# Two-layer decoder step on one core: the second root of four norm pairs moves from the tokens to the finished tiles of the projection that follows

## The reference, cut to what matters

```python
def rmsnorm(x, g):
    return x * lax.rsqrt(jnp.mean(x * x, -1, keepdims=True) + EPS) * g
# layer l
x = x + rmsnorm(m, norm_mix_post[l])            # m: what the mixer gave
h = rmsnorm(x, norm_x_pre[l])
x = x + rmsnorm(cross_attend(h, mem_k, mem_v, wq, wo), norm_x_post[l])   # q = h @ wq
h = rmsnorm(x, norm_ffn_pre[l])
f = swiglu(h, wg, wu, wd)                       # (silu(h @ wg) * (h @ wu)) @ wd, layer 0
x = x + rmsnorm(f, norm_ffn_post[l])
h = rmsnorm(x, norm_mix_pre[l + 1])
# mixer of layer 1
q, f, i, g = split(h @ w_in, 4)
fg = lb + (1 - lb) * sigmoid(f);  qh = silu(q);  kh = 1 - fg;  lf = log(fg)
bc = cumsum(lf);  q_in = qh * exp(bc);  k_in = kh * exp(-bc)   # in chunks of 64 tokens
```

## Time and profile before

| | |
|---|---|
| median of three runs | 2251.37 us |
| profiled execution, device time | 2249.11 us |
| span of its trace, first to last instruction | 2246.8 us |
| mean granted clock of TensorE | 0.922 of full speed |
| TensorE busy | 2047.6 us |
| VectorE busy | 1494.1 us |
| ScalarE busy | 1218.5 us |
| GpSimd busy | 132.8 us |

### The profile page before, as it was taken

One profiled execution on the slowest core, in us unless ns is written; L12 is line 12 of the kernel. 1 busy time (PEld: TensorE's weight loads), 2 busy tenths in 40 slices (PEclk: granted clock), 3 DMA queues, 4 the chain that ended last, 5 costly groups with the idle time before them and its releaser, 6 DMA issues.

```text
span 2246.8 us, 29766 instructions
## 1 busy us (share of the span) xinstructions
PE 2047.6 (91%) x10660; PEld 1667.6 (74%) x10660; DVE 1494.1 (66%) x2113; ACT 1218.5 (54%) x1620; POOL 132.8 (6%) x160
## 2 busy tenths in 40 slices
PE   7999998888899978797987899999999999999993
PEld 6774647757799878746656688888888888888882
DVE  2413734562655354475544799999999999999994
ACT  3321213433444435313323788888878788887883
POOL 2000300000000000041000000000000000000001
PEclk9999997888899988768877899999999999999996
DMA  6324665364455473244542999999999999999991
GB/s 155 117 95 157 216 199 197 114 206 149 132 176 172 141 267 127 85 131 174 187 164 72 384 379 375 373 374 381 373 380 366 382 370 388 368 385 370 382 370 68
DMA packets 234941, 556.03 MB, mean 247 GB/s; under 512 B 10534, under 2 KB 13826, under 8 KB 234854
## 3 DMA queue, kind: packets, MB, share of 16 engines
q1 hardware_dynamic: 213422, 474.87, 59.2%
q0 software_dynamic: 21440, 80.07, 10.5%
HBM read 525.38 MB, written 29.62 MB: 247 GB/s over the span
## 4 chain that ended last, share of the span: by engine, by line
PE 78%; DVE 11%; DMA 5%; ACT 3%; issue 2%; POOL 1%; DVEq 0%; ACTq 0%; POOLq 0%
PE banks L1320 9%; PE banks L1322 9%; PE banks L1321 9%; PE banks L793 6%; PE banks L794 5%; PE banks L795 5%; PE banks L763 5%; PE banks L823 5%; PE banks L1313 5%; PE banks L1311 5%; PE banks L1312 5%; PE banks L844 2%; DVE arena L1978 1%; DVE weight_parts L1703 1%; PE banks L1330 1%
## 5 line engine op out<-in xcount | busy, mean ns | idle before, releaser
L2270 DVE TENSOR_TENSOR weight_parts<-arena,weight_parts 128x1024 fp32r<-128x1024 f32 x672 | 799.9, 1222 | 64.3 <-ACT weight_parts L1653 32.7
L1653 ACT ACTIVATE weight_parts<-arena 128x1024 fp32r<-128x1024 f32 x672 | 700.9, 1061 | 141.3 <-PE banks L1322 90.5
L1320 PE MATMUL banks<-weight_parts,token_parts 128*128 128x512 f32 x896 | 356.2, 398 | 6.3 <-DVE weight_parts L2270 6.3
L1322 PE MATMUL banks<-weight_parts,token_parts 128*128 128x512 f32 x896 | 350.1, 391 | 0.0
L1321 PE MATMUL banks<-weight_parts,token_parts 128*128 128x512 f32 x896 | 349.7, 390 | 0.0
L793 PE MATMUL banks<-token_parts,weight_parts 128*128 128x264 f32 x992 | 295.2, 298 | 48.9 <-DVE token_parts L1737 16.7
L1703 DVE TENSOR_TENSOR weight_parts<-arena,weight_parts 128x1024 fp32r<-128x1024 f32 (+1 forms) x158 | 186.2, 1195 | 193.2 <-ACT weight_parts L1357 177.1
L1357 ACT ACTIVATE weight_parts<-arena 128x1024 fp32r<-128x1024 f32 (+1 forms) x158 | 162.8, 1037 | 275.9 <-PE banks L795 195.0
L794 PE MATMUL banks<-token_parts,weight_parts 128*128 128x264 f32 x992 | 292.6, 295 | 0.0
L795 PE MATMUL banks<-token_parts,weight_parts 128*128 128x264 f32 x992 | 291.9, 294 | 0.0
L793 PEld LDWEIGHTS banks<-token_parts,weight_parts 128*128 128x128 f32 x992 | 198.2, 200 | 52.8 <-DVE weight_parts L1703 29.0
(11 more groups left out here) (441 smaller groups left out, 2443.8 us busy)
## 6 DMA issues: line engine op xcount, KB each, us to landing
arena<-in_moe_w_gate SPq DMA_DIRECT2D x112, 1024.0 KB, 7.6
arena<-in_moe_w_up SPq DMA_DIRECT2D x112, 1024.0 KB, 8.0
arena<-in_moe_w_down SPq DMA_DIRECT2D x112, 1024.0 KB, 7.4
arena<-in_ev_w_in SPq DMA_DIRECT2D x18, 1024.0 KB, 5.0
arena<-in_cache_mem_k POOLq DMA_DIRECT2D x16, 1024.0 KB, 6.0
arena<-in_cache_mem_v POOLq DMA_DIRECT2D x16, 1024.0 KB, 5.4
arena<-in_od_w_in SPq DMA_DIRECT2D x16, 1024.0 KB, 5.9
arena<-in_ffn_w_gate SPq DMA_DIRECT2D x10, 1024.0 KB, 5.1
```

What stands on the lines that cost most here:

```text
L1320: mm(out, xh, hi[:, cols], start=(c == 0), stop=False)
L1322: last = mm(out, xl, hi[:, cols], start=False, stop=(c == DC - 1))
L1653: f(wr_[:, q % QRING, 0, :], quarter(q), ACT.Copy).then_inc(S("hi_made"), 1)
L2270: TT(wr_[:, q % QRING, 1, :], quarter(q), wr_[:, q % QRING, 0, :].bitcast(F32), ALU.subtract) \
```

## The change

At the four pairs the second root is no longer multiplied into the tokens. The parts of the tokens are made from X times gain, without the root, as soon as X is updated: ScalarE makes the high part beside the square of the chunk, and VectorE the low part with one operation, X times gain less the high part. The projection multiplies these, and since the root is one number per token, it multiplies the finished tile instead: VectorE now empties the tiles of `q`, `gate`, `up`, `f`, `q`, `i` and `g` with a multiplication by the root (`times_rs`). Where an activation follows, ScalarE applies it to the emptied tile (`activate`). In the feed-forward the root belongs in two places, ahead of SiLU and on the product, so VectorE multiplies a gate tile by it once more after SiLU. The sums of squares of the second norm stand inside the projection: two chunks after the first quarter of its first column block, two after the second quarter, four ahead of the last quarter.

```diff
-            plan(f"q{l}", 8), plan(f"qs{l}", 2), ...
+            plan(f"q{l}", 8, "v"), plan(f"qs{l}", 2), ...
-                plan("f", 8), plan("q", 8), plan("i", 8), plan("g", 8)
+                plan("f", 8, "v"), plan("q", 8, "v"), plan("i", 8, "v"), plan("g", 8, "v")
@@ TensorE
-            def project_split(name, cols, hi_x, lo_x, ready=None, chunks=DC):
+            def project_split(name, cols, hi_x, lo_x, ready=None, chunks=DC, sums=None):
...
+                        if sums is not None and c0 == 0 and k0 == 6:
+                            square_sum(sums, 4), square_sum(sums, 5), square_sum(sums, 6), square_sum(sums, 7)
                         pe.wait_ge(lo_made, q + 1)
...
+                        if sums is not None and c0 == 0 and k0 < 4:
+                            square_sum(sums, k0), square_sum(sums, k0 + 1)
...
-                square_sums(k_pre)
-                project_split(f"q{l}", D, token_hi, token_lo, parts_of(f"q{l}"))
+                project_split(f"q{l}", D, token_hi, token_lo, parts_of(f"q{l}"), sums=k_pre)
...
@@ ScalarE
+            def activate(x, fn, name, c):
+                act.wait_ge(empty["v"], emptied(n_of(name, c))[1])
+                f(x, x, fn).then_inc(S("activated"), 1)
...
             def squares_of_x(k):
                 for c in range(DC):
                     act.wait_ge(S("x_updated"), DC * posts.index(k - 1) + c + 1)
+                    if k in SPLIT_NORMS:
+                        f(x_hi[:, c, :], XT[:, c, :], ACT.Copy, scale=gain(kind, layer, c)).then_inc(S("x_hi_made"), 1)
                     f(MT[:, c, :], XT[:, c, :], ACT.Square).then_inc(S("squares_ready"), 1)
...
             def attention(l, k_post, k_pre):
+                first_hi(f"q{l}")
                 root(k_post)
                 squares_of_x(k_pre)
-                first_hi(f"q{l}")
+                hi_ahead(n_of(f"q{l}", 0), 2)
                 root(k_pre)
-                input_hi(k_pre)
-                for c in range(DC):
-                    b = tile(n_of(f"q{l}", c))
-                    f(QT[:, c, :], b[:, 0:T], ACT.Copy, scale=(D // XH) ** -0.5).then_inc(empty["a"], 1)
+                hi_ahead(n_of(f"q{l}", 7))
...
+            for c in range(DC):
+                hi_ahead(n_of("f", c))
+                activate(Fg[:, c, :], ACT.Sigmoid, "f", c)
             act.wait_ge(S("fg_ready"), 1)
             f(Fg, Fg, ACT.Ln).then_inc(S("logf_ready"), 1)
-            for c in range(DC):
-                b = tile(n_of("i", c))
-                f(I[:, c, :], b[:, 0:T], ACT.Copy).then_inc(empty["a"], 1)
+            hi_ahead(n_of("f", 7), 4)
             act.wait_ge(S("bc_ready"), 1)
...
+            for c in range(DC):
+                hi_ahead(n_of("q", c))
+                activate(Q[:, c, :], ACT.Silu, "q", c)
...
@@ VectorE
                 link(v.reciprocal(rs, rs))
+                if k in SPLIT_NORMS:
+                    return
...
+                        if c >= 3 and k + 1 in SPLIT_NORMS:
+                            dve.wait_ge(S("x_hi_made"), PARTS[SPLIT_NORMS[k + 1]] + c - 2)
+                            STT(out=x_lo[:, c - 3, :], in0=XT[:, c - 3, :], scalar=gain(next_kind, next_layer, c - 3),
+                                in1=x_hi[:, c - 3, :].bitcast(F32), op0=ALU.mult, op1=ALU.subtract).then_inc(S("x_lo_made"), 1)
+            def times_rs(name, c, out):
+                b = tile(n_of(name, c))
+                return TT(out, b[:, 0:T], rs, ALU.mult)
...
+                first_lo(f"q{l}")
                 finish_norm(k_post)
-                first_lo(f"q{l}")
+                lo_through(f"q{l}", 0)
                 finish_norm(k_pre)
-                lo_through(f"q{l}", 7)
+                for c in range(DC):
+                    b = tile(n_of(f"q{l}", c))
+                    STT(out=QT[:, c, :], in0=b[:, 0:T], scalar=(D // XH) ** -0.5, in1=rs, op0=ALU.mult, op1=ALU.mult) \
+                        .then_inc(empty["v"], 1)
...
+            for i, n in enumerate(FGROUPS):
+                for j in range(n):
+                    times_rs(f"gate{i}", j, gtmp[j]).then_inc(empty["v"], 1)
+                for j in range(n):
+                    lo_through(f"gate{i}", 3 if n == 4 else 1, 2)
+                    dve.wait_ge(S("activated"), 4 * i + j + 1)
+                    TT(gtmp[j], gtmp[j], rs, ALU.mult).then_inc(S("dve_step"), 1)
...
+            for c in range(DC):
+                times_rs("f", c, Fg[:, c, :]).then_inc(empty["v"], 1)
+            dve.wait_ge(S("activated"), FC + DC)
...
+            for c in range(DC):
+                times_rs("q", c, Q[:, c, :]).then_inc(empty["v"], 1)
+            lo_through("q", 7, 4)
             dve.wait_ge(S("e_ready"), 1)
...
```

More of the change, by code:

```diff
@@ L455, in program @@
         posts = [n for n, (_, _, pre) in enumerate(NORMS) if not pre]
-        PRES = [n for n, (_, _, pre) in enumerate(NORMS) if pre]
+        NORMED = [n for n, (_, _, pre) in enumerate(NORMS) if pre and n not in SPLIT_NORMS]
         block = ctx.enter_context(nc.Block())
@@ L837, in transposes, with square_sum @@
                 last.then_inc(tile_done, 1)
+            def square_sum(k, c):
+                pe.wait_ge(S("squares_ready"), DC * k + c + 1)
+                sq = MT if NORMS[k][2] else HT
+                last = mm(ps[:, 4, 0:T], ones, sq[:, c, :], start=(c == 0), stop=(c == DC - 1))
+                if c == DC - 1:
+                    last.then_inc(S("square_sums_done"), 1)
             def square_sums(k):
                 for c in range(DC):
-                    pe.wait_ge(S("squares_ready"), DC * k + c + 1)
-                    sq = MT if NORMS[k][2] else HT
-                    last = mm(ps[:, 4, 0:T], ones, sq[:, c, :], start=(c == 0), stop=(c == DC - 1))
-                last.then_inc(S("square_sums_done"), 1)
+                    square_sum(k, c)
             def wait_norm(k, chunks=DC):
-                pe.wait_ge(S("normed"), DC * PRES.index(k) + chunks)
+                pe.wait_ge(S("normed"), DC * NORMED.index(k) + chunks)
             pe.wait_ge(S("consts_ready"), 1)
@@ L1135, in attention @@
                 square_sums(k_pre + 1)
-                square_sums(k_pre + 2)
+                if l == 1:
+                    square_sums(k_pre + 2)
             attention(0, 1, 2)
             for i, n in enumerate(FGROUPS):
-                project_split(f"gate{i}", n * P, token_hi, token_lo, parts_of("gate0") if i == 0 else None)
+                project_split(f"gate{i}", n * P, token_hi, token_lo, parts_of("gate0") if i == 0 else None, sums=4 if i == 0 else None)
                 project_split(f"up{i}", n * P, token_hi, token_lo)
@@ L1144, in _ @@
             square_sums(5)
[L1145 to L1147 removed]
+            project_split("f", D, token_hi, token_lo, parts_of("f"), sums=6)
             project_split("q", D, token_hi, token_lo)
@@ L1544, in attention @@
                 block_out(f"xo{l}")
-                root(k_pre + 1)
                 if l == 0:
                     first_hi("gate0")
+                root(k_pre + 1)
                 squares_of_x(k_pre + 2)
+                if l == 0:
+                    hi_ahead(n_of("gate0", 0), 2)
                 root(k_pre + 2)
-                if l == 0:
-                    input_hi(k_pre + 2)
             attention(0, 1, 2)
@@ L1555, in _ @@
                 for j in range(n):
-                    b = tile(n_of(f"gate{i}", j))
-                    if i:
-                        act.wait_ge(empty["v"], emptied(n_of(f"up{i - 1}", j))[1])
-                    f(gtmp[j], b[:, 0:T], ACT.Silu).then_inc(empty["a"], 1)
+                    hi_ahead(n_of(f"gate{i}", j))
+                    activate(gtmp[j], ACT.Silu, f"gate{i}", j)
                 for j in range(n):
@@ L1728, in finish_norm @@
                 link(v.reciprocal(rs, rs))
+                if k in SPLIT_NORMS:
+                    return
                 if pre:
[L1730 to L1738 removed]
+                    for c in range(DC):
+                        STT(out=HT[:, c, :], in0=XT[:, c, :], scalar=gain(kind, layer, c), in1=rs,
+                            op0=ALU.mult, op1=ALU.mult).then_inc(S("normed"), 1)
                 else:
[L1740 removed]
+                    for c in range(DC + 3):
                         if c < DC:
@@ L2080, in _ @@
             last.then_inc(S("e_used"), 1)
+            for c in range(4):
+                times_rs("i", c, I[:, c, :]).then_inc(empty["v"], 1)
             dve.wait_ge(S("e_ready"), 3)
             TT(K[pr], K[pr], E[pr], ALU.mult).then_inc(S("k_decayed"), 1)
+            for c in range(4, DC):
+                times_rs("i", c, I[:, c, :]).then_inc(empty["v"], 1)
+            for c in range(DC):
+                times_rs("g", c, G[:, c, :]).then_inc(empty["v"], 1)
             lo_through("g", 7)
```

77 lines of the change are left out of this document (35 added, 42 removed).

## The result

The changed kernel takes 2215.56 us (median of four runs, 2215.14 to 2217.78) against 2250.5 beside it: ratio 0.9857, 95% interval 0.9843 to 0.9872. Timed a second time on another occasion it gave 2215.64 us and 0.9872 (0.985 to 0.9894). So it is faster, by about 32 us by the ratio and 34.9 between the medians, where 2230 was forecast. The profiled execution took 2215.14 us, with a span of 2213.4.

The account below looks back on a forecast made before the run. TensorE, busy 91% of the span, was taken as the bound, so only its stops could yield time: 2.7 + 3.4 + 14.6 + 2.7 - 3.5 = 19.9 us off 2249.1, given as 2230 us, range 2217 to 2245.

Parts of the forecast that it names:

- those of 9.9 and 8.5 us: TensorE's stops between f and g before the change, at 806.8 and 902.5, because ScalarE empties tiles late.
- The pair: Norm pairs: projection starts 9.2 us earlier, new 2.4 us stop; net 2.7 us at q0 and q1, 3.4 at gate0.
- Clock charge: After the new stops at three places the clock may fall, costing 2.4 us; half charged, 3.5 us together.
- f to g: From f's first block to g's end, a chain on three engines: g ends 14.6 us earlier, the largest term.
- The stops of 7.5 and 4.6: TensorE's predicted stops in us ahead of the second blocks of q and i, with none ahead of g's.
- the edits that it costs at nothing: VectorE's two extra operations per hidden feed-forward tile, GpSimd's memsets and SP's later requests, all charged no time.
- The zeros win: Rival, f to g: q's two weight blocks land at 14.4 us each, second at 832.3; 2240 to 2243; chance 0.15.
- The feed-forward: Rival: TensorE waits at each of six groups for gate's trip between VectorE and ScalarE; 2259 us; chance 0.04.
- No hiding: Rival: sums, later wait and clock give back all at q0, gate0, q1; f to g gains half; 2242; chance 0.09.
- The rival at 2219: Rival: zeros cost q nothing and the clock holds at the three stops; about 2219 us; chance 0.1.

Follow-up runs that it names:

- lo_before_root: Changed kernel, but VectorE makes the two low weight parts ahead of the wait for the second root at the four pairs: 2207.7 us, ratio 0.9809.
- both_edits: Changed kernel with low weight parts ahead of the second root and the zeros in eight pieces during the feed-forward: 2201.42 us, ratio 0.9791.
- zeros_again: Changed kernel with the 8 MB of zeros in eight pieces during the feed-forward, timed once more: 2214.69 us, ratio 0.9862.

## Why the prediction came out as it did

- **Direction and bound: right.** TensorE's stops were the place. Of the four that it names from f to g, those of 9.9 and 8.5 us went as described; 26.0 us of stops became 18.4.
- **The pair: right.** First matmul 5.68 us behind the sums (5.7 forecast), stop of 2.32 (2.4), ended by VectorE's first emptying. The three pairs ahead of `q0`, `gate0` and `q1` gave 6.4 us together, where the sum had 5.3 with the clock charged.
- **Clock charge: near in sum, open in kind.** The forecast took a fall at 2.4 us, from a block that begins after a pause, and half of it at three places, 3.5. The falls happened at two of the three and made the block behind 1.5 us longer (13.42 against 11.92). Whether that is a cost on top is open: without the stops lo_before_root got back no more than the stops, both_edits 1.4 to 1.5 us more at `q0` and at `gate0`.
- **f to g: mechanism right, size 2.8 short.** The stops of 7.5 and 4.6 were 6.10 and 4.55. Ahead of those the forecast's times leave stops of 2.6 ahead of q and 3.1 ahead of its third quarter; there was one of 5.41 ahead of the third quarter. q's two blocks were ready 35.7 and 45.6 us behind `down`'s end, where 39.8 and 47.5 were forecast, so the sigmoids and all behind them came 1.9 earlier. It is in part luck that this is so near: the first block took 6.1 us where 11 were forecast, and the second landed 10.0 behind it where 7.7 were, two errors that go against each other. What the forecast did not say is that 8 of the 17.4 us are the zeros' new place and would go to any kernel that moves them.
- **What failed: a term that is not in the sum.** The attentions stand neither in the sum nor among the edits that it costs at nothing. The step "VectorE now empties the tiles" was followed into its projection alone. Each emptying also makes the weight parts that run ahead of it, so two low parts of `xo` left the attention's chain, some 2.3 us twice, shown by the two kernels that move only them. With 1.6 us of clock in the second attention, whose cause is open, and 1.2 that no run assigns, the attentions are 7.3 of the 13.5 us between forecast (19.9) and traces (33.4). Then 2.8 from f to g, 1.1 at the pairs, and 2.3 in stages that the change leaves alone.
- **Rivals.** "The zeros win" is refuted by the landings: q's second block was ready 45.6 us behind `down`'s end, not 57.6. The feed-forward does not wait: 960 matmuls from `up0` to the last `up` in 118.68 us against 116.95, and the difference is the clock behind the stop (117.17 in lo_before_root, without it). "No hiding" fell with the 5.68 and 2.32 us. The rival at 2219 comes nearest in time, but neither of its conditions held: the zeros still took 4.4 us from f to g, and the clock fell at two of the three stops.

## What to carry to other kernels

When an engine takes over an operation, follow all that its helper does on the way (here the weight parts made ahead), into the stage behind and not only in the one that is changed. Ask of a stop that a late transfer ends whether the waiting engine needs that transfer yet: one quarter less lead removed a stop of 9.9 us, of which 5.6 were left at f's end and 2.8 at g's, and one large fill cut in pieces and spread over a stage with spare transfer time took 12.5 us off the stage in which it had stood.

## What was not expected of the hardware

Eight transfers of 1 MB between weight blocks left the weights' median landing at 5.3 us. Beside one transfer of 8 MB it was the order of the requests that told: a block asked for 0.2 us behind it landed after 6.1 us and the 8 MB waited, while the two blocks asked for 4 to 10 us behind it took 12.0 and 15.3 us in the changed kernel, 14.4 and 18.3 in the kernel before. And a stop of 2.32 us was followed by a fall of the clock at two of four places with the same instructions in the changed kernel's trace, and at three of the four in that of zeros_again.
